# First block's second dense stage as five 1024-column units of seven half-size products, with left operands kept in DRAM

## The reference

```python
h = _rmsnorm(x, pre_g)
proj = jnp.einsum('bld,de->ble', h, w_in)
z_ssm, xbc, dt_raw, q, k, v, f_raw, z_att, g_ssm, g_att = jnp.split(proj, ...)
xbc = silu(_causal_dwconv(xbc, conv_w, conv_b))
y = _ssd_chunked(xs, dt, a, b_ssm, c_ssm, d_skip)
yg = y * silu(z_ssm); yg = yg * rsqrt(mean(yg*yg per group of 256) + eps)
y_ssm = yg * ssm_norm_g
o = _forgetting_attention(heads(q), heads(k), heads(v), log_f)
y_att = o * silu(z_att)
p_ssm = y_ssm @ w_branch_ssm;  p_att = y_att @ w_branch_att
merged = sigmoid(g_ssm) * p_ssm + sigmoid(g_att) * p_att
x = x + _rmsnorm(merged @ w_out, post_g)
```

## Time and profile before

| | us |
|---|---|
| median of 3 runs | 2918.06 |
| lowest and highest | 2914.38, 2933.96 |
| profiled execution, span | 2928.2 |
| PE busy | 2774.1 (95%) |
| DVE, ACT, POOL busy | 1895.8, 1450.4, 519.0 |
| first dense stage, from and to | 25 to 262 |
| stage `bs`, from and to | 372 to 876 |
| attention | 876 to 1157 |

### The profile page before, as it was taken

The page is one execution under the profiler, slowest core; times in us unless marked ns, Lnnn a source line. Parts: engine busy times, 40 slices in busy tenths (PEclk is TensorE's granted clock), DMA queues, the critical chain, the costliest instruction groups (busy, mean ns, idle before and its releaser), DMA issues.

```text
span 2928.2 us, 36019 instructions
## 1 busy us (share of the span) xinstructions
PE 2774.1 (95%) x13406; PEld 2270.3 (78%) x13406; DVE 1895.8 (65%) x2160; ACT 1450.4 (50%) x2147; POOL 519.0 (18%) x394
## 2 busy tenths in 40 slices
PE   7999999999998999999989998999999899999997
PEld 6788977888876776887878886778778788887875
DVE  4776745443445564344543887899773798888886
ACT  4444435423435665344333347633432377777774
POOL 0001400000005776001000000000010144434332
PEclk9998999999998999999999998999999899999999
DMA  4110021213447673121211110111222699999995
GB/s 104 43 44 15 1 60 44 101 44 108 163 129 179 140 153 89 54 84 67 88 63 47 44 36 1 30 44 51 94 87 96 227 383 371 372 366 365 364 360 188
DMA packets 162601, 387.94 MB, mean 132 GB/s; under 512 B 72321, under 2 KB 72449, under 8 KB 137888
## 3 DMA queue, kind: packets, MB, share of 16 engines
q1 hardware_dynamic: 151920, 369.13, 37.7%
q0 software_dynamic: 9216, 16.81, 2.3%
q10 hardware_dynamic: 1328, 0.14, 0.0%
HBM read 347.93 MB, written 54.85 MB: 138 GB/s over the span
## 4 chain that ended last, share of the span: by engine, by line
PE 52%; DMA 12%; DVE 8%; ACT 5%; POOL 5%; issue 4%; POOLq 0%; DVEq 0%; ACTq 0%; SPq 0%; PEldq 0%
PE ps L897 12%; PE ps L899 12%; PE ps L898 12%; DMA ex_raw<-in_w_up_e 9%; POOL fa_pl L1336 5%; DMA ex_raw<-in_w_down_e 3%; DVE ex_w L3130 3%; PE ps L2980 2%; ACT ex_w L3065 2%; PE ps L2708 1%; PE ps L1741 1%; PE ps L2710 1%; PE ps L1743 1%; PE ps L1742 1%; PE ps L2709 1%
## 5 line engine op out<-in xcount | busy, mean ns | idle before, releaser
L3130 DVE TENSOR_TENSOR ex_w<-ex_raw,ex_w 128x2048 fp32r<-128x2048 f32 x190 | 430.9, 2289 | 64.7 <-ACT ex_w L3065 62.6
L3065 ACT ACTIVATE ex_w<-ex_raw 128x2048 fp32r<-128x2048 f32 x190 | 362.3, 1917 | 118.6 <-DMA ex_raw<-in_w_up_e 65.2
L2980 PE MATMUL ps<-ex_w,ex_xT 128*128 128x512 f32 x1536 | 368.2, 396 | 13.8 <-DVE ex_xT L3145 13.8
L2980 PEld LDWEIGHTS ps<-ex_w,ex_xT 128*128 128x128 f32 x1536 | 286.8, 190 | 80.5 <-issue 15.0
L1003 DVE TENSOR_TENSOR bs_t<-arena,bs_t 128x1024 fp32r<-128x1024 f32 x88 | 107.7, 1224 | 269.5 <-ACT bs_t L956 269.4
L956 ACT ACTIVATE bs_t<-arena 128x1024 fp32r<-128x1024 f32 x88 | 93.4, 1061 | 294.2 <-PE ps L899 280.4
L793 DVE SCALAR_TENSOR_TENSOR arena<-arena,small 128x1023 f32<-128x1023 f32 (+9 forms) x168 | 213.4, 1271 | 3.5
L1336 POOL TENSOR_TENSOR fa_pl<-fa_p,fa_ph 128x512 fp32r<-128x512 f32 x192 | 196.1, 1039 | 82.6 <-ACT fa_ph L1474 79.3
L2980 PE MATMUL ps<-ex_w,ex_hT 128*128 128x512 f32 x768 | 182.9, 394 | 0.8 <-issue 0.7
L897 PE MATMUL ps<-bs_t,bs_w 128*128 128x512 f32 x448 | 175.4, 391 | 7.8 <-DVE bs_w L994 4.2
L899 PE MATMUL ps<-bs_t,bs_w 128*128 128x512 f32 x448 | 174.4, 389 | 0.0
(11 more groups left out here) (425 smaller groups left out, 6604.1 us busy)
## 6 DMA issues: line engine op xcount, KB each, us to landing
ex_raw<-in_w_gate_e SPq DMA_DIRECT2D x64, 1024.0 KB, 13.8
ex_raw<-in_w_up_e SPq DMA_DIRECT2D x64, 1024.0 KB
ex_raw<-in_w_down_e SPq DMA_DIRECT2D x64, 1024.0 KB, 14.1
arena<-in_w_in SPq DMA_DIRECT2D x108, 512.0 KB, 3.7
att_qk<-bs_split SPq DMA_DIRECT2D x8, 2048.0 KB, 11.0
fa_a<-att_qk SPq DMA_DIRECT2D x32, 256.0 KB
fa_b<-att_qk SPq DMA_DIRECT2D x16, 512.0 KB, 6.5
arena<-in_w_out SPq DMA_DIRECT2D x16, 512.0 KB, 6.1
```

The lines of the kernel that those rows point to most:

```text
L2980: mm = nc.tensor.matmul(out, l, r, start=(k == 0 and n == 0), stop=(k == kc - 1 and n == 2))
L3065: nc.scalar.activation(half_of(part[m][0], h), raw[m][:, h * W // 2: (h + 1) * W // 2], ACT.Identity).then_inc(high[m], 1)
L3130: V.tensor_tensor(half_of(part[m][1], h), raw[m][:, h * W // 2: (h + 1) * W // 2], half_of(as_f32(part[m][0]), h), ALU.subtract)\
```

## The change

In stage `bs`, `phase_dense` is replaced by `phase_units`. A full unit is 1024 columns of weights by 1024 tokens with both operands cut in halves: seven half-size products (Strassen's scheme in Winograd's form), each of 4 steps, each step 4 tiles by three matmuls. A half unit (g_ssm) has the four ordinary half products. Units in order: z (full), g_ssm (half), q, k, v, branch (full): 156 steps of 12 matmuls.

- **Left operands** A11, A12, A22 and the sums S1 to S4 (and A21 for the half unit) are kept in DRAM as high and low parts. For `h` they are made in the first dense stage (`KeptOperands`): SP stores the rounded parts of `hT` from its steps 0 to 7, and ACT waits for that store before it overwrites the slot; POOL makes 16 sums and their 16 low parts, ACT their high parts, one each step from step 4, SP stores them. `hT` itself is stored too (4 MB). For `y` they are made in stage `bs` (`MadeOperands`), one every second step from step 48, with two slots, high parts by ACT, low parts by DVE, sums by POOL, store by SP four steps later.
- **In each step** SP loads one operand of 128x1024 (four slots), ACT rounds one 128x512 chunk of weights, DVE makes its low part (three slots). Weights come as four quarters of 1 MB into region 0, over `hT`. DVE combines quarters in place: 16 operations per full unit.
- **Evictions.** After products 1, 3 and 4 of a full unit ACT copies four tiles (`tapped`), after 2, 5, 6 and 7 DVE adds or subtracts the banks (`joined`). Split units then make high and low parts again from SBUF, 16 by ACT and 16 by DVE, and SP stores each quarter, 2 MB, after waiting for the low parts. The first tap of a unit waits until the unit before has its low parts stored. The branch unit's products with the gate are 16 POOL operations.
- **Gating** spreads over steps 30 to 46; transposes stand before step 44.
- **Attention**: POOL's fills follow its products; `hT` is loaded back from DRAM after `load_v(0)`, and the `za` stage waits for it.

```diff
@@ phase_dense
                 if fetch is not None and u in fetch:
                     fetch[u](sp)
+                if keep is not None:
+                    keep.sync(sp, u, t_low, both)
...
+                if keep is not None:
+                    keep.before_step(act, n)
@@ new
+    def before_step(self, act, n):
+        if 2 <= n < KC + 2:
+            act.wait_ge(self.raw_kept[n % 2], 32 * (n // 2))
...
+        make(0)
+        for k in range(CH):
+            if k + 1 < CH:
+                make(k + 1)
+            for x in range(4 * k, 4 * k + 4):
+                both = self.both[x % self.RING]
+                pool.wait_ge(self.high, x + 1)
+                T(both[:, 1, :], self.sums[k % 2][x % 4], both[:, 0, :].bitcast(F32), ALU.subtract)\
+                    .then_inc(self.low, 1)
...
+FULL = (("A11", "B11", 0, True), ("A12", "B21", 1, True), ("S2", "B11", 0, False), ("S3", "B12", 0, False),
+        ("A22", "B21", 1, True), ("S1", "B12", 0, True), ("S4", "B22", 0, False))
+HALF = (("A11", "B11", 0, True), ("A12", "B21", 0, False), ("A21", "B11", 1, True), ("A22", "B21", 1, False))
+TAPS = {0: (0, 0), 2: (0, 1), 3: (1, 1)}
+JOINS = {1: (0, 0), 4: (1, 0), 5: (1, 1), 6: (0, 1)}
...
+        def load_operand(n):
+            u, x = products[n // 4]
+            if n >= NA:
+                multiplied_by(sp, n - NA)
...
+        def load_later(n):
+            for q in QUADS:
+                for before, u in zip(loads[q], loads[q][1:]):
+                    free = step0[before] + freed_at[full[before]][q]
+                    if n == free + 2:
+                        sp.wait_ge(low, free + 1)
+                        load_weights(u, q)
+
+        def store(n):
+            for u in splits:
+                for i, (x, (r, s)) in enumerate(JOINS.items()):
+                    if n == step0[u] + 4 * x + 3 + 5:
+                        sp.wait_ge(split_low, split0[u] + 4 * (i + 1))
+                        to_high, to_low = units[u].stores(r, s)
+                        sp.dma_start(to_high, staged(u, i).bitcast(F32)).then_inc(kept[i % 2], 16)
+                        sp.dma_start(to_low, units[u].other[1](r, s).bitcast(F32)).then_inc(low_kept, 16)
...
+        for n in range(NS + 8):
+            if NA <= n < NS:
+                load_operand(n)
+            load_later(n)
+            store(n)
+            if at is not None:
+                at(sp, n, tail)
...
+        for n in range(NS + 4): 
+            if n < NS:
+                round_weights(n)
+            if n >= 2 and n - 2 < NS and (n - 2) % 4 == 3:
+                take(n - 2)
+            if n >= 3 and n - 3 < NS and (n - 3) % 4 == 3:
+                finish(n - 3)
+            if beside is not None:
+                beside(n, opened)
...
+        for n in range(NS + 4): 
+            if n + 1 < NS:
+                combine(n + 1)
+            if n < NS:
+                low_weights(n)
+            m = n - 2
+            if 0 <= m < NS and m % 4 == 3:
+                join(m)
+            m = n - 3
+            if 0 <= m < NS and m % 4 == 3:
+                finish(m)
+            if aside is not None:
+                aside(n, opened)
@@ GatedTurn
-    STEP, BY_ACT = 3 * KC, (1, 4, 7, 10, 12, 14)
+    FIRST, TURN, BY_ACT = 30, 44, (1, 4, 7, 10, 12, 14)
@@ phase_forget_attention
             load_v(0)
+            sp.wait_ge(tail.low, tail.steps)
+            sp.dma_start(hT, hT_kept).then_inc(h_back, 16)
```

565 lines of the change are left out of this document (481 added, 84 removed).

## The result

The changed kernel takes 2960.78 us (median; 2960.26 to 2964.42) against 2917.57 us of the kernel before beside it (2914.38 to 2933.96): the ratio is 1.0138, 95% interval 1.0108 to 1.0167. It is slower by 1.4%, where 2901 us and no measurable change were forecast, and it lies above the range's end of 2942.

What follows compares the result with a forecast made beforehand. PE was taken to set the pace in the changed stage, with DMA room. Terms -60.2 + 37 - 5 + 3 + 4 + 2 + 2 + 0 = -17 us gave 2901 us on the median 2918.1; range 2865 to 2942.

Steps and rivals of the forecast that it cites:

- Products removed: In the changed stage, 240 fewer matmuls (1872 instead of 2112) at 0.2267 us each: -54.4 us.
- Drains: Consecutive units change banks and no longer drain: ten boundaries by 0.58 us, -5.8 us.
- DMA stalls: Bursts at unit turns (+12, +12, +5) and late second-product stores (+3, +3, +2): +37 us, ends 5 to 75.
- 7 made 9.0: In the burst from q to k, seven stores of operands made from y take 9.0 of 51.2 us of queue.
- rival C: DVE and ACT cannot keep a 2.72 us step in q, k and v: 2951 us, chance 0.08.
- DVE and POOL: First dense stage: new POOL operations slow DVE's beside them by about 1.1 us each; +4 us, 0 to 16.
- Clock: Lower granted clock at two boundaries where PE is busy about 75% of 35 us: +2 us.
- ACT around the gating: Roundings and squares spread over eight 2.72 us steps end PE's loss before the gating's turn: -5 us.
- Start: The first PE step waits for 1.57 MB instead of 0.52, and steps 1 to 4 for more loads: +3 us.
- POOL in the stage: In the changed stage, 16 sums and the branch unit's 16 products fall mostly into DVE's lead: +2 us.
- DVE's worst place: Steps 9 to 11 of q, k, v: 15 us of DVE work leaves 0.5 us before PE waits; counted zero.
- Attention: hT reloaded from DRAM and value slots filled 4 us later do not delay the attention: 0, -2 to +4 us.

Runs made afterwards that it cites:

- e8: e7 with the 28 operands made from y bunched into steps 48 to 64, 79 to 93 and 107 to 115: 2920.2 us, ratio to before 0.9978.
- e2: The changed kernel with a third slot for the operands made from y: 2941.0 us, ratio to before 1.0061.
- e5: The changed kernel with a third slot, first-dense-stage sums and low parts on DVE, and taps waiting per stored quarter: 2930.1 us, ratio to before 1.0015.
- e7: e5 with the stores of q, k and v issued from ACT's queue: 2907.4 us, ratio to before 0.9929; timed again, 0.9963.
- e12: e7 with three quarters of the bytes of q's, k's and v's stores left out: 2891.4 us.
- e4: The changed kernel with the first dense stage's sums and low parts of kept operands on DVE instead of POOL: 2947.9 us, ratio to before 1.0074.

## Why the prediction was wrong, step by step

**Products removed, -54.4.** Right to the tenth: 1872 matmuls, 0.2267 us apart. **Drains, -5.8**: no gap stands at a boundary for them.

**DMA stalls, +37.** The bytes were right (147.4 MB, 145 counted) and so was the rate in full stretches (378 to 397 GB/s over 32 to 45 us of mixed reads and writes, 410 over 16 us of e8, against 410 assumed). The size was nearly right as well, but only for a kernel whose other waits are out of the way: in e2 the gaps that end with an operand's load are 48.3 us (42.2 for h, 6.1 for y), of which 3.5 belong to the start. The places were foreseen too. In e5 the turn from q to k has 11.4 us of gaps (five, from 580.6 to 614.6), k to v 12.4 and v to the branch unit 4.7, forecast at +12, +12 and +5; operand 13, behind the store of the second product, has 4.5, 4.5 and 1.2, forecast at +3, +3 and +2. What the sum lacked are 5.3 us (4.5 in after) behind the attention's loads in the branch unit. In after itself only 24 us of gaps are DMA's by name, since another wait came first. The Trainium skill (DMA: Bandwidth & Descriptors, Specifications) gives about 358 GB/s for a core; the 397 GB/s over 45 us in e7 are above it, so here the measurement decides.

**The step that failed: made operands counted as bytes.** The sum had "7 made 9.0" us in the queue and nothing else. It did not ask what waits for such a store. With two slots and a job every second step, a slot is wanted again after 2 x 5.44 = 10.9 us. But SP takes a job's store up four steps after the job: over the 28 jobs of after the median is 7.6 us from the start of the high part to the issue of the store. Then it lands in 8.5 (median; 5.0 to 12.7), together 16.1 for 10.9. So ACT waited in 24 of 26 jobs, also where the queue was calm: 2.1 us at 543.86, behind a store that landed after 5.1. Even the 3.7 us of a load alone do not fit into the 3.3 that are left. In the case shown it was 11.0 us to the issue, 4.3 of them SP's own wait for q's low parts, and 8.3 to the landing, behind 2 MB of q; the earlier trace rows has 8.6 to 14.1 us for stores of 2 MB, so it could be seen there that a store behind them lands late. Late by 4.3 us on average and by 10.6 at most, it holds ACT at L1183, and in ACT's order behind it stand the rounding of the weights and the taps; DVE's low part and joins stand behind ACT. The prediction named "late stores of made operands" in rival C, at 8% and as a term of DVE's step only. That mechanism, on ACT, made +24 us (e2), and the total went past C's 2951. Whether issuing the made stores two steps sooner would have done what the third slot did is not tested.

This step and the one on DVE and POOL below together put the result outside the range: with the third slot alone the kernel is at 1.0061 of before, with the sums on DVE alone at 1.0074, some 2935 and 2939 us on the median of before, and either would have lain inside 2865 to 2942, yet slower than before and not faster.

**Clock, +2.** Measured 22.2 us against 1.8 before, +20. The forecast argued from "PE busy about 75% of 35 us at two boundaries"; what the traces show is that single short stalls suffice. In after, 12 stretches of 2.5 to 5.5 us run at twice the pitch, eleven of them behind a gap of 2.5 us or more and one at the stage's start, each costing 1.1 to 2.6 us. The other half of the argument, "where DMA sets the pace a slower PE costs nothing", was not tested by itself: where the gaps shrank, so did the slow stretches, and both came off the stage (21.1 and 5.6 us in e12). Part of this loss in after stands behind stalls of the failed step above, so it is a consequence and not a third cause; in e2 it is 13.7, in e7 10.3, in e12 4.7.

**DVE and POOL, +4, bounds 0 to 16.** Measured at the end of the first dense stage: some 8 us (9.1 between after and e4), twice the term and inside the bounds. The stores of that stage, counted as zero, are at most the 2 us that stay with the sums on DVE. The mechanism was right and the size off: the sum took three places where something waits (1 + 2 + 1), while DVE as a whole lost more there, (1039 - 684) x 39 = 14 us on the weights' low parts alone, and its lead absorbed only part of it. The Trainium skill (SBUF — State Buffer, SBUF: two separate sides) has the lock of the port pair for such a pair of operations, and for VectorE's operations in a two-port mode beside them; the trace agrees (1039 ns against 684, and 1004 against 808 for L791, which has one array as input). The forecast's 1.1 us for each POOL operation was read from operations with two array inputs only.

**ACT around the gating, -5.** Right: no gap but the turn's own stands between 410 and 524.5, and the turn keeps its shape, 8.8 us (9.4 before). **Start, +3**: 2.5 us at 407.9; another 3.4 us before the first matmul (11.5 us later at the state-space stage's start, 14.9 at this one's) lie within the 109.2 to 116.3 us that this stretch takes in the changed kernels, and stay without a cause. **POOL in the stage, +2**: not told apart. **DVE's worst place, zero**: 9 us of gaps end with a low part of DVE's (the chain leads from the 3.4 us at 627.6 back to the store at 614.88); with the third slot 1.4 are left. **Attention, 0**: 4 us less from the stage's end to the kernel's end; other kernels with the same code there have -8 to +3 against before, so nothing shows.

In sum, in the profiled executions: -54.4 for the products, gaps +56.7 (of which about 29 at taps and joins and 24 at loads), clock +20.4, small change +1.0, which is the stage's +23.7; the stage's start +14.9; the rest -4.2; together +34.4. The forecast had -17: -21 for the stage and +4 ahead of it. Of the difference, 51.6 us before rounding, the third slot takes 23.8 (stalls and the clock behind them). Another 21.1 are what the stage of e2 has above its forecast: 8 of DMA stalls (44.8 instead of 37), 10 of slow clock, 3 of small gaps. Ahead of the stage 10.9 are above the term, of which GpSimd's neighbourhood explains about 4, and 4.2 come off again behind the stage. The 9 us by which the medians' difference exceeds the profiles' are the spread of single executions (2914.4 to 2934.0 us for before); no cause was looked for.

## What to carry to other kernels

For each ring of slots that a DMA empties, write down the time after which a slot is wanted again. Against it set the time from filling the slot to the issue of its store, plus the landing under the heaviest traffic of that stretch, not the alone one; then list what stands behind the engine that waits. Price a stall of 3.4 us or more on TensorE with another 1 to 2.6 us of slow matmuls behind it, and count shorter ones, from 2 us on, as open. Keep urgent loads behind neither a wait nor a large transfer on their issuing engine: moving the stores from SP to ACT gave 21 us here, while moving the same bytes in time gave nothing.
